# Two attention halves in a fused layer kernel: projections two steps ahead, logits one step ahead, two buffers for the soft logits

## What is computed

```python
def hybrid_layer(x, w_in, w_out, ln_g, ln_b, rel_bias, topk):
    proj = jnp.einsum('bsd,dn->bsn', x, w_in)
    qA, kA, vA, gA, qB, kB, vB, gB, qI, kI, wI = jnp.split(proj, SPLIT_POINTS, axis=-1)
    oA = stick_breaking_attention(qA, kA, vA)              # 8 heads, each of 64
    oB = dsa_sparse_attention(qB, kB, vB, qI, kI, wI, rel_bias, topk)
    mix = jnp.concatenate([oA * jax.nn.silu(gA), oB * jax.nn.silu(gB)], axis=-1)
    return layer_norm(ALPHA * x + jnp.einsum('bsm,md->bsd', mix, w_out), ln_g, ln_b)
```

## Time and profile before

| | us |
|---|---|
| median of 3 runs | 2979.33 |
| lowest, highest | 2976.88, 2986.76 |
| the profiled execution | 2977.58 |
| its span, first to last instruction | 2975.8 |
| group stage 0 | 1601 to 2168 |
| group stage 1 | 2168 to 2663 |
| group stage 2 | 2663 to 2976 |

### The profile page before, as it was taken

How to read it: one execution, slowest core, us unless ns; L and a number is a source line. 1 busy time by engine, 2 the same in 40 slices (tenths; PEclk the granted TensorE clock), 3 DMA queues, 4 the chain that set the end, 5 groups by cost and what they waited for, 6 DMA issues and landing times. The chain is left out here.

```text
span 2975.8 us, 30375 instructions
## 1 busy us (share of the span) xinstructions
PE 2398.3 (81%) x9779; PEld 1605.8 (54%) x9779; DVE 1751.3 (59%) x3656; ACT 908.0 (31%) x1740; POOL 987.2 (33%) x691
## 2 busy tenths in 40 slices
PE   6997999869878898898786986797566467559897
PEld 4776878758663343343333664575345336337575
DVE  3444311032136988988975688587759869755151
ACT  4444222233322222222222443243133324323232
POOL 2332555343232343344342234234323523310001
PEclk9998999989998999999898997899678678759898
DMA  4321333223139899999999899899799999964553
GB/s 158 97 67 50 98 98 101 81 81 126 49 121 347 314 406 415 416 409 402 395 410 405 333 379 372 314 371 394 295 355 384 416 409 398 380 260 172 216 190 140
DMA packets 257323, 805.56 MB, mean 271 GB/s; under 512 B 18366, under 2 KB 139862, under 8 KB 191655
## 3 DMA queue, kind: packets, MB, share of 16 engines
q0 software_dynamic: 73728, 536.90, 44.8%
q1 hardware_dynamic: 183463, 267.06, 25.6%
HBM read 795.07 MB, written 14.07 MB: 272 GB/s over the span
## 5 line engine op out<-in xcount | busy, mean ns | idle before, releaser
L1337 POOL DMA_INDIRECT gathered<-in_peer_rows,experts x436 | 532.5, 1221 | 918.2 <-DVE x_res L2635 607.0
L1695 PE MATMUL peer_banks<-gathered,peer_diags 128*128 128x512 f32 x720 | 338.3, 626 | 56.2 <-ACT peer_diags L1750 56.2
L78 PE MATMUL group_banks<-group_x_t,group_ring 128*128 128x128 f32 (+1 forms) x2016 | 338.1, 331 | 16.7 <-ACT group_x_t L2447 8.4
L2621 DVE CUSTOM_DVE_ANT_0 gathered<-gathered,late_nat 128x1024 f32<-128x1024 f32 x256 | 317.8, 1244 | 35.0 <-DMA gathered<-in_peer_rows,experts 29.9
L2635 DVE SCALAR_TENSOR_TENSOR x_res<-gathered,group_weights,x_res 128x1024 f32<-128x1024 f32 x256 | 331.4, 1295 | 2.7 <-DVE group_weights L2627 0.3
L78 PEld LDWEIGHTS group_banks<-group_x_t,group_ring 128*128 128x128 f32 x2016 | 305.4, 207 | 46.3 <-ACT group_x_t L2447 10.8
L1695 PEld LDWEIGHTS peer_banks<-gathered,peer_diags 128*128 128x128 f32 x720 | 142.2, 201 | 241.7 <-issue 241.7
L2261 PE MATMUL group_banks<-group_ring,group_x_t 128*128 128x512 f32 x512 | 233.7, 611 | 28.4 <-DMA group_ring<-in_weights 28.4
L1790 DVE CUSTOM_DVE_ANT_0 peer_product<-gathered,early_nat 128x1024 f32<-128x1024 f32 x180 | 214.7, 1222 | 37.9 <-DMA gathered<-in_peer_rows,experts 36.6
L1695 PE MATMUL peer_banks<-early_gathered,peer_diags 128*128 128x512 f32 x304 | 149.3, 643 | 51.7 <-ACT peer_diags L1750 51.7
L2261 PEld LDWEIGHTS group_banks<-group_ring,group_x_t 128*128 128x128 f32 x512 | 98.3, 197 | 150.2 <-issue 117.0
(11 more groups left out here) (376 smaller groups left out, 4201.6 us busy)
## 6 DMA issues: line engine op xcount, KB each, us to landing
group_ring<-in_weights SPq DMA_DIRECT2D x270, 512.0 KB, 4.7
mixer_wq<-in_w_in SPq DMA_DIRECT2D x24, 512.0 KB, 4.1
mixer_wk<-in_w_in SPq DMA_DIRECT2D x24, 512.0 KB, 4.1
peer_w<-in_w_pq SPq DMA_DIRECT2D x8, 1024.0 KB
gathered<-in_peer_rows,experts POOLq DMA_INDIRECT x436
diff_wv<-in_w_in SPq DMA_DIRECT2D x8, 512.0 KB, 4.0
conv_wb<-in_w_in SPq DMA_DIRECT2D x8, 512.0 KB, 4.0
merge_w<-in_w_conv_out SPq DMA_DIRECT2D x8, 512.0 KB
```

The lines of the kernel that those rows point to most:

```text
L78: last = nc.tensor.matmul(out, lhsT, rhs, start=n == 0, stop=n == len(pairs) - 1)
L1337: nc.gpsimd.indirect_dma_start(row_buffer(m, r), None, A["peer_rows"], bass.IndirectOffsetOnAxis(ap=at, axis=0))\
L1695: last = nc.tensor.matmul(ps[:, ACC[unit % 2] + half, :], diags[:, r % DIAGS, :], row_buffer(m, r)[:, D + half * BANK:D + (half + 1) * BAN ...
L2621: nc.vector.tensor_tensor_reduce(out=row, in0=row, in1=m.late_nat[:, t % 2, :], scale=1.0, scalar=0.0, op0=ALU.mult, op1=ALU.add, accum_ou ...
```

## The change

It reorders the programs of TensorE and ScalarE in the group stage and the lists that go with them. VectorE's order stays. The soft logits get a second place: `near_part(u)` is 0 for even and 2 for odd pairs, and `suffix` gets two halves. In the stick half TensorE's order is now, for each u: logits u+1, tails u, pair u+2, output u; pair 1 is projected before the stick gates. In the sparse half: logits u+1, transposes u, pair u+2, output u; so pair 6 is projected before the sparse gates. ScalarE runs softplus u+1 before the weights of u, copies pair u+2 after them, and makes the exponentials of the sparse unit u+1 in the middle of unit u. The last bias is loaded when pair 7 is done and no longer when pair 6 is. The lines of the lists, of SP, TensorE and ScalarE:

```diff
@@ -1846,9 +1846,9 @@
     def quarters_of(kind, name):
         return [(kind, name, b) for b in range(4)]
 
-    return [("kI",)] + [("qI", n) for n in range(4)] + quarters_of(STICK, "v") + pair(STICK, 0) + quarters_of(STICK, "g") \
-        + pair(STICK, 1) + pair(STICK, 2) + pair(STICK, 3) + pair(SPARSE, 0) + quarters_of(SPARSE, "v") + pair(SPARSE, 1) \
-        + quarters_of(SPARSE, "g") + pair(SPARSE, 2) + pair(SPARSE, 3) + [("out", c) for c in range(KC)]
+    return [("kI",)] + [("qI", n) for n in range(4)] + quarters_of(STICK, "v") + pair(STICK, 0) + pair(STICK, 1) + quarters_of(STICK, "g") \
+        + pair(STICK, 2) + pair(STICK, 3) + pair(SPARSE, 0) + quarters_of(SPARSE, "v") + pair(SPARSE, 1) \
+        + pair(SPARSE, 2) + quarters_of(SPARSE, "g") + pair(SPARSE, 3) + [("out", c) for c in range(KC)]
 
 
 WEIGHTS = weight_order()
@@ -1993,6 +1993,10 @@
     def pair_banks(u):
         return 2 + 2 * (u % 2)
 
+    def near_part(u):
+
+        return 2 * (u % 2)
+
     with ctx:
         ps = banks()
         ring = sb("ring", [P, WS, D])
@@ -2137,7 +2141,7 @@
                         store_values(l, SPARSE)
                     if b == WEIGHTS.index((SPARSE, "g", 3)):
                         load_bias(l, 2)
-                    if b == WEIGHTS.index((SPARSE, "k", 2)):
+                    if b == WEIGHTS.index((SPARSE, "k", 3)):
                         load_bias(l, 3)
                     if b == WEIGHTS.index(("out", 3)):
                         if keeps:
@@ -2399,22 +2403,24 @@
                     index_scores(l)
                     pair(l, 0)
                     stick_logits(l, 0)
+                    pair(l, 1)
                     natural(l, "g", STICK)
                     for u in range(PAIRS):
-                        pair(l, u + 1)
-                        tails(l, u)
                         if u + 1 < PAIRS:
                             stick_logits(l, u + 1)
                         else:
+                            sparse_logits(l, PAIRS)
+                        tails(l, u)
+                        if u + 1 == PAIRS:
                             natural(l, "v", SPARSE)
-                            sparse_logits(l, PAIRS)
+                        pair(l, u + 2)
                         stick_out(l, u)
                     for u in range(PAIRS, UNITS):
                         if u + 1 < UNITS:
-                            pair(l, u + 1)
+                            sparse_logits(l, u + 1)
                         turn_weights(l, u)
-                        if u + 1 < UNITS:
-                            sparse_logits(l, u + 1)
+                        if u + 2 < UNITS:
+                            pair(l, u + 2)
                         if u == PAIRS:
                             natural(l, "g", SPARSE)
                         sparse_out(l, u)
@@ -2571,36 +2577,36 @@
                     copy_pair(l, 0)
                     done = gelus((l, "pair0"), done)
                     softplus(l, 0)
+                    copy_pair(l, 1)
                     done = gelus((l, "soft0"), done)
                     done = gates(l, STICK, done)
                     for u in range(PAIRS):
                         done = gelus((l, "stick", u, 0), done)
-                        copy_pair(l, u + 1)
-                        stick_weights(l, u)
-                        done = gelus((l, "stick", u, 1), done)
                         if u + 1 < PAIRS:
                             softplus(l, u + 1)
-                        else:
+                        done = gelus((l, "stick", u, 1), done)
+                        stick_weights(l, u)
+                        if u + 1 == PAIRS:
                             done = copy_values(l, SPARSE, done)
+                        copy_pair(l, u + 2)
                         done = gelus((l, "stick", u, 2), done)
                         done = gelus((l, "stick", u, 3), done)
                     done = gelus((l, "keep"), done)
+                    sparse_weights(l, PAIRS)
                     for u in range(PAIRS, UNITS):
                         p = u - PAIRS
+                        if p:
+                            done = gelus((l, "sparse", p, 0), done)
+                        copy_turned(l, u)
+                        if u + 2 < UNITS:
+                            copy_pair(l, u + 2)
                         if p == 0:
-                            sparse_weights(l, u)
-                            copy_pair(l, u + 1)
-                            copy_turned(l, u)
                             done = gates(l, SPARSE, done)
                             done = gelus((l, "gate1"), done)
                             copy_mix(l, STICK)
-                        else:
-                            sparse_weights(l, u)
-                            done = gelus((l, "sparse", p, 0), done) if p else done
-                            if u + 1 < UNITS:
-                                copy_pair(l, u + 1)
-                            copy_turned(l, u)
                         done = gelus((l, "sparse", p, 1), done)
+                        if u + 1 < UNITS:
+                            sparse_weights(l, u + 1)
                         done = gelus((l, "sparse", p, 2), done)
                         done = gelus((l, "sparse", p, 3), done)
                     copy_mix(l, SPARSE)
```

16 lines of the change are left out of this document (8 added, 8 removed).

## The result

The changed kernel takes 3016.8 us (median of 4 runs, 3005.0 to 3028.1), against 2978.1 for the kernel before: ratio 1.0123, 95% interval 1.0094 to 1.0153. It is slower by 38.6 us, the forecast's sum; the interval leaves 28 to 46 us open. Timed again (the last experiment), it came to 1.0131 (1.0116 to 1.0147).

The account below looks back on a forecast made before the run. VectorE's queue was taken to bound groups 0 and 1, TensorE group 2. Stick end 4.0, last bias with VectorE's delay 21.9 and group 2 12.7 sum to 38.6 us, giving 3017 us, range 2981 to 3048.

Parts of the forecast that it names:

- the forecast's sum: All six layer passes of the group stage: later gelus, bias loads and group 2 chains together add 38.6 us.

Follow-up runs that it names:

- the last experiment: The changed kernel measured once more, unedited, against the kernel before: 1.0131 (1.0116 to 1.0147), median 3016 us.
- two edits: Changed kernel with the last bias loaded right behind the third (1.0075), or with pair 6 projected behind the sparse gates again (1.0114); both together 1.0004.

## What to carry to other kernels

Work moved in front of a stage moves every load whose place in a queue is tied to that work: put each load at the point where its own needs are met, and the same reorder costs 1.0022 in place of 1.0127. (The 1.0004 needed pair 6 back behind the gates as well.) Costs can hide each other, and gains too: two edits that give 15 and 4 us alone gave 36 together, and the stick half and the earlier third bias, each worth nothing alone (1.0009, 1.0011), gave 0.9979. So a suspected pair is tested as a pair. And before you give a wait a value, ask what stands right behind the engine that it waits for.

## What the runs showed of the hardware

- The last bias took 5 to 6 us from issue to landing with no gathers (group 2), 5.4 and 7.9 where POOL stood still just before or during the load (group 1 of the changed kernel), and 16 to 22 while gathering went on (group 0, third bias early). Taking one wait out of POOL's program put another of its size behind the next load (10.8 us gone, 11.3 new, group 1, layer 1).
- While both queues had work they moved the same number of packets (557 and 556 in 13 us), so the one with the larger packets got three times the bytes (4.05 and 1.33 MB).
- Three idle gaps of 1.1 to 2.4 us within 12 us of TensorE's work stood ahead of a fall of its clock, and the 16 output matmuls then took 3.67 us and not 1.89. In the kernel before gaps of 1.49, 0.31 and 1.11 us did (3.09 us), and with the longest gap taken away (both late biases earlier) the clock fell all the same. Which gap is to blame no run isolates.
